# Gate and up of a feed-forward stage: one 512-column product for the high weights

## The chip, the core and the metric

The kernel runs on one core of a Trainium2 chip. The metric is the device time of one launch in microseconds, a median over runs. Lower is better.

## What is computed

A block with a state-space branch, attention and 32 experts (the first part), and then four layers, each with a mixer and a SwiGLU feed-forward stage. D is 1024, there are 256 tokens, and the hidden width is 2816. The change touches the four feed-forward stages alone:

```
def _swiglu(xn, w_gate, w_up, w_down):
    return (jax.nn.silu(xn @ w_gate) * (xn @ w_up)) @ w_down

for i in range(4):
    ...                                   # mixer: m
    x = x + _rms(m, g[1])
    f = _swiglu(_rms(x, g[2]), ffn_w_gate[i], ffn_w_up[i], ffn_w_down[i])
    x = x + _rms(f, g[3])
```

Everything is in 32 bits. The late products split each operand into a high part (rounded to the type fp32r) and a low part (the rest), and add three products: high weight with high input, high weight with low input, low weight with high input.

## The kernel before

**Layout.** Channels lie on the 128 partitions, tokens (256) along the free dimension. x is 8 chunks of 128 x 256. A piece of weights is 128 x 2048, 1 MB, and holds 16 blocks of 128 x 128. PSUM has 8 banks of 512 columns; `halves(b)` sees bank b as two outputs of 256 columns.

**A feed-forward stage** (`ffn`, L897) takes 33 pieces. For each index i of 11 (256 hidden channels) there is a gate piece, an up piece and a down piece; the order is gate 1, up 1, gate 2, up 2, down 1, and from then on gate i+1, up i+1, down i. The middle eight indices run in a hardware loop of two each (`FFN_TRIPS`), the last pieces are gate 11, up 11, down 10, down 11. `hidden_pair` (L901) makes gate and up: for each of the 8 input chunks k and both output halves m it calls `product` (L451), three products of 256 columns into one half of a bank:

```
mm(out, w[0], a[0], start=start, stop=False, **more)
mm(out, w[0], a[1], start=False, stop=False, **more)
return mm(out, w[1], a[0], start=False, stop=stop, **more)
```

Gate i goes to bank 4 or 5 in turn, up i to 6 or 7; the down pieces add into banks 0 to 3. Each product loads its weight block itself. After the first gate piece TensorE sums the squares of x (`x_sums`, L471), from which ACT makes `rstd_x`.

**Engines beside TensorE.** SP loads pieces into a ring of six slots, piece n when piece n-6 has been read (`late`). ACT makes the high part of a piece (`late_first`, L1152), DVE the low part from it (`low_part`, L361, called by `late_second`), four pieces ahead. Between these, in a fixed order, they treat the hidden values: DVE scales gate with `rstd_x` (`f_g`), ACT takes silu (`gate_silu`, L1287), DVE scales up (`f_u`) and multiplies (`f_a`), ACT makes the high part of that (`hidden_first`, L1291) and DVE the low part (`hidden_second`, semaphore `f_low`), on which the down piece waits. For each index ACT's order is: high part of a piece, silu, high part, hidden high, high part; DVE's: low part, f_g, low part, f_u and f_a, low part, hidden low. Ahead of the stage, `add_result` on DVE and `next_input` on ACT (L1173) make the input's parts `h2` chunk by chunk, and the first gate piece waits for each chunk.

**Memory.** `h2` has its high part in `h_parts` and its low part at 4096 of the arena; `squares` lies at 2048 of the arena.

Of the kernel before, what the change touches and what calls it, by code (L numbers as in the profile page):

```python
# [16 lines left out]
T = 256  # L17
# [179 lines left out]
def build(nc, io):  # L197
    with ExitStack() as ctx:
# [127 lines left out]
        h2 = (shaped(h_parts[:], (KC, T)), parts(4096, KC, T))  # L326
# [19 lines left out]
        f_a = view(7680, 2, T)  # L346
        f_parts = tuple(parts(8192 + 1024 * n, 2, 2, T) for n in range(2))
# [95 lines left out]
        def _(pe):  # L443
# [17 lines left out]
            def norm_sums(b):  # L461

                k = at["norm"]
                for c in range(KC):
                    if c % 2 == 0:
                        pe.wait_ge(sem("squares_ready"), 4 * k + c // 2 + 1)
                    last = mm(psum[:, b, 0:T], ones, squares[:, c, :], start=c == 0, stop=c == KC - 1)  # L467
                last.then_inc(sem("norm_sums"), 1)
                at["norm"] += 1
# [313 lines left out]
            norm_sums(4)  # L783
# [50 lines left out]
            def diff_attention(ready):  # L834
# [57 lines left out]
                for head in range(HEADS2):  # L892
                    pe.wait_ge(sem("o2_ready"), head + 1)
                    for c in range(2):
                        last = mm(halves(2, 2)[:, head, :], ones, squares[:, 2 * head + c, :], start=c == 0, stop=c == 1)
                last.then_inc(sem("o2_sums"), 1)
            def ffn(layer):  # L897
# [44 lines left out]
            for layer in range(LAYERS):  # L942
                ready = (sem("late_h_low"), MIXER_H[layer] * KC)
                if layer == 1:
                    norm_sums(5)
# [12 lines left out]
                norm_sums(2)  # L958
                ffn(layer)
                norm_sums(4)  # L960
# [5 lines left out]
        def _(act):  # L966
# [13 lines left out]
            def squares_of(src, waits=None):  # L980
                if at["norm"] >= 1:
                    act.wait_ge(sem("norm_sums"), at["norm"])
                for n in range(4):
# [3 lines left out]
                    go(squares[:, cols, :], src[:, cols, :], ACT.Square).then_inc(sem("squares_ready"), 1)  # L987

            def x_squares():

                at["x"] += 1
                squares_of(x, (sem("x_ready"), KC * (at["x"] - 1)))
# [176 lines left out]
            for j in range(4):  # L1169
                go(squares[:, 2 * j:2 * j + 2, :], halves(j), ACT.Square).then_inc(sem("squares_ready"), 1)  # L1170
            rstd_of(4)

            def next_input(scales):  # L1173
# [3 lines left out]
                for c in range(KC):  # L1177
                    act.wait_ge(sem("x_ready"), KC * (at["x"] - 1) + c + 1)
                    go(h2[0][:, c, :], x[:, c, :], ACT.Copy, scale=scales[:, c:c + 1]).then_inc(sem("late_h_high"), 1)
                    if c % 2:  # L1180
                        go(squares[:, c - 1:c + 1, :], x[:, c - 1:c + 1, :], ACT.Square).then_inc(sem("squares_ready"), 1)

            def result_out(i, done, scales=None):
# [3 lines left out]
                if scales is None:  # L1187
                    go(squares[:, 2 * i:2 * i + 2, :], halves(i % 2), ACT.Square).then_inc(sem("squares_ready"), 1)
                    go(mixed[:, 2 * i:2 * i + 2, :], halves(i % 2), ACT.Copy).then_inc(sem("pair_out"), 1)
                    return  # L1190
                for fn, dst, signal in ((ACT.Square, squares, "squares_ready"), (ACT.Copy, mixed, "pair_out")):
# [4 lines left out]
            for layer in range(LAYERS):  # L1196
# [13 lines left out]
                elif layer == 1:  # L1210
                    x_squares()
# [8 lines left out]
                else:  # L1220
# [23 lines left out]
                    for i in range(HEADS2 * TT):  # L1244
# [8 lines left out]
                        if i % TT == TT - 1:  # L1253
# [3 lines left out]
                            go(squares[:, 2 * head:2 * head + 2, :], o2[:, 2 * head:2 * head + 2, :], ACT.Square  # L1257
# [28 lines left out]

                def gate_silu(i):  # L1287
# [7 lines left out]
                for i in range(2):  # L1295
                    late_first(n + AHEAD + 2 * i)
                    gate_silu(it + 1 + i)
                    late_first(n + AHEAD + 2 * i + 1)
                    hidden_first(it + 1 + i, i)
                late_first(n + AHEAD + 4)  # L1300
                m = n + FFN_HEAD + AHEAD
                with act.Fori(0, FFN_TRIPS) as i:
                    for buf in range(2):
                        late_first(m + 3 * buf, i)
                        gate_silu(i * 2 + (it + 3 + buf))
                        late_first(m + 3 * buf + 1, i)
                        hidden_first(i * 2 + (it + 3 + buf), buf)
                        late_first(m + 3 * buf + 2, i)
                m = n + FFN_PIECES
                late_first(m)  # L1310
                gate_silu(it + FC2)
                late_first(m + 1)
                hidden_first(it + FC2, 0)
# [4 lines left out]
                for j in range(4):  # L1318
# [4 lines left out]
                    go(squares[:, 2 * j:2 * j + 2, :], halves(j), ACT.Square).then_inc(sem("squares_ready"), 1)  # L1323
# [761 lines left out]
```

## Time and profile before

| | us |
|---|---|
| median of 3 runs | 2685.67 |
| lowest, highest | 2682.75, 2690.65 |
| the profiled execution | 2689.83 |
| its span, first to last instruction | 2688.0 |
| mean granted TensorE clock | 0.957 |
| TensorE busy (share of the span) | 2476.4 (92%) |
| DVE busy, ACT busy | 1124.7, 691.9 |

The first product of the four layers starts at 1460.90 us of the span, and the four feed-forward stages fill most of what follows. A timeline row gives the start, the duration, the engine, the line, the operation, and output<-inputs with their shapes; in brackets stands how long the engine was idle before it, and what ended that. A product's duration overlaps the next one's: the pace is read from the distance of the starts. PE is TensorE's product, PEld its weight load.

### The profile page before, as it was taken

How to read it: one execution, taken by the hardware profiler on the slowest of the kernel's cores; microseconds unless marked ns; L12 is line 12 of the kernel's file. 1: busy time of each engine (PE TensorE's matmuls, PEld its weight loads, DVE VectorE, ACT ScalarE, POOL GpSimd, SP SyncE). 2: the span in 40 equal slices, each digit the busy share in tenths (PEclk: the TensorE clock that was granted, in tenths of full speed). 3: DMA queues.
4: the chain of work that ended last, by engine and by line, in shares of the span. 5: the costliest groups of instructions: out<-in, count | busy, mean ns of one | idle time of the engine just before them, and what ended most of it. 6: DMA issues, size and time to landing. Idle time of an engine off the chain costs nothing.

```text
span 2688.0 us, 37887 instructions
## 1 busy us (share of the span) xinstructions
PE 2476.4 (92%) x15414; PEld 1799.1 (67%) x15414; DVE 1124.7 (42%) x1599; ACT 691.9 (26%) x855; POOL 95.1 (4%) x52
## 2 busy tenths in 40 slices
PE   7866888999999999999997999969999899998998
PEld 4544764444444444444445989959999789988998
DVE  5876312111111111111114755565555455566553
ACT  1122120000000000000003344344343444344432
POOL 0123000000000000000000000000000000000000
PEclk9877987999999999999998999989999899999999
DMA  7333326999999999999995444524544145444552
GB/s 314 110 111 147 121 84 274 422 422 422 422 422 422 422 422 422 422 421 422 422 422 236 171 158 180 187 78 169 187 172 157 59 145 187 176 154 141 173 187 79
DMA packets 93764, 676.41 MB, mean 252 GB/s; under 512 B 10452, under 2 KB 11096, under 8 KB 11640
## 3 DMA queue, kind: packets, MB, share of 16 engines
q1 hardware_dynamic: 92592, 673.36, 63.4%
q10 hardware_dynamic: 1096, 1.97, 0.2%
q8 instruction: 55, 0.90, 0.1%
q14 instruction: 21, 0.17, 0.0%
HBM read 674.23 MB, written 1.06 MB: 251 GB/s over the span
## 4 chain that ended last, share of the span: by engine, by line
PE 74%; DMA 13%; DVE 9%; ACT 2%; issue 1%; POOL 0%; SPq 0%; DVEq 0%; ACTq 0%; POOLq 0%
PE psum L715 13%; PE psum L453 13%; PE psum L454 12%; PE psum L455 12%; DMA ring<-in_w_exp 12%; PE psum L740 5%; DVE arena L1373 3%; PE psum L699 3%; PE psum L513 3%; PE psum L467 2%; DVE arena L1379 2%; PE psum L750 2%; PE psum L633 1%; PE psum L494 1%; PE psum L603 1%; DVE arena_parts L1379 1%
## 5 line engine op out<-in xcount | busy, mean ns | idle before, releaser
L454 PE MATMUL psum<-arena_parts,ring_parts 128*128 128x256 f32 x2832 | 809.8, 286 | 0.0
L453 PE MATMUL psum<-h_parts,ring_parts 128*128 128x256 f32 x1920 | 555.7, 289 | 39.3 <-DVE arena_parts L1379 38.2
L454 PEld LDWEIGHTS psum<-arena_parts,ring_parts 128*128 128x128 f32 x2832 | 552.8, 195 | 0.2
L364 DVE TENSOR_TENSOR ring_parts<-ring,ring_parts 128x2048 fp32r<-128x2048 f32 x181 | 414.4, 2291 | 322.5 <-ACT ring_parts L1162 317.2
L455 PE MATMUL psum<-h_parts,ring_parts 128*128 128x256 f32 x1920 | 548.3, 286 | 0.0
L715 PE MATMUL psum<-ring,arena 128*64 128x512 f32 x2176 | 486.4, 597 | 5.4 <-DMA ring<-in_w_exp 5.3
L453 PEld LDWEIGHTS psum<-h_parts,ring_parts 128*128 128x128 f32 x1920 | 374.0, 195 | 49.3 <-issue 32.0
L455 PEld LDWEIGHTS psum<-h_parts,ring_parts 128*128 128x128 f32 x1920 | 374.1, 195 | 0.0
L1162 ACT ACTIVATE ring_parts<-ring 128x2048 fp32r<-128x2048 f32 x181 | 342.2, 1903 | 70.8 <-DMA ring<-in_w_mix 47.0
L715 PEld LDWEIGHTS psum<-ring,arena 128*64 128x64 f32 x2176 | 152.1, 137 | 296.6 <-issue 296.6
L1376 DVE TENSOR_SCALAR arena<-psum 128x512 f32<-128x512 f32 x68 | 47.0, 691 | 627.9 <-ACT arena L1141 469.8
L453 PE MATMUL psum<-arena_parts,ring_parts 128*128 128x256 f32 x912 | 261.9, 287 | 29.7 <-DVE arena_parts L1373 29.7
L455 PE MATMUL psum<-arena_parts,ring_parts 128*128 128x256 f32 x912 | 261.0, 286 | 0.0
L740 PE MATMUL psum<-ring,arena 128*64 128x512 f32 x1088 | 241.0, 595 | 0.0
L453 PEld LDWEIGHTS psum<-arena_parts,ring_parts 128*128 128x128 f32 x912 | 178.3, 196 | 31.3 <-issue 25.7
L740 PEld LDWEIGHTS psum<-ring,arena 128*64 128x64 f32 x1088 | 75.1, 137 | 161.7 <-issue 161.7
L455 PEld LDWEIGHTS psum<-arena_parts,ring_parts 128*128 128x128 f32 x912 | 178.2, 195 | 0.0
L699 PEld LDWEIGHTS psum<-arena 128*128 128x128 f32 x1120 | 130.9, 196 | 31.1 <-issue 31.1
L699 PE MATMUL psum<-arena 128*128 128x64 f32 x1120 | 135.8, 281 | 3.4 <-DVE arena L1376 3.4
L1135 ACT ACTIVATE arena<-psum 128x512 f32<-128x512 f32 x35 | 20.9, 597 | 374.4 <-PE psum L699 374.4
L1373 DVE TENSOR_TENSOR arena<-psum,rstd_x 128x512 f32<-128x512 f32 x112 | 77.0, 688 | 86.4 <-PE psum L455 86.4
L1373 DVE TENSOR_TENSOR arena<-arena 128x512 f32<-128x512 f32 (+6 forms) x160 | 103.5, 651 | 9.8 <-ACT arena L1006 4.7
(245 smaller groups left out, 1977.4 us busy)
## 6 DMA issues: line engine op xcount, KB each, us to landing
ring<-in_w_exp SPq DMA_DIRECT2D x408, 1024.0 KB, 19.0
ring<-in_w_ffn SPq DMA_DIRECT2D x132, 1024.0 KB, 4.8
ring<-in_w_mix SPq DMA_DIRECT2D x49, 1024.0 KB, 4.8
ring<-in_w_ada SPq DMA_DIRECT2D x24, 1024.0 KB, 5.1
ring<-in_w_in SPq DMA_DIRECT2D x16, 1024.0 KB, 6.2
ring<-in_w_out SPq DMA_DIRECT2D x4, 1024.0 KB, 4.8
ring<-in_w_attn SPq DMA_DIRECT2D x2, 1024.0 KB, 4.7
ring<-in_w_ssm SPq DMA_DIRECT2D x2, 1024.0 KB, 5.5
```

The lines of the kernel that those rows point to most:

```text
L364: return engine.tensor_tensor(ring_parts[:, s, :], ring[:, s, :], ring_parts[:, RAW + s, :], ALU.subtract)
L453: mm(out, w[0], a[0], start=start, stop=False, **more)
L454: mm(out, w[0], a[1], start=False, stop=False, **more)
L455: return mm(out, w[1], a[0], start=False, stop=stop, **more)
L467: last = mm(psum[:, b, 0:T], ones, squares[:, c, :], start=c == 0, stop=c == KC - 1)
L513: last = mm(halves(n % 2)[:, m, :], blocks_of(slot)[:, m * KC + k, :], src[:, k, :], start=k == 0, stop=k == KC - 1)
L699: last = mm(psum[:, 6, m * CAP:(m + 1) * CAP], h_tok[:, t, m * P:(m + 1) * P], sel[:, t, :], start=t == 0, stop=t == TT - 1)
L715: last = mm(psum[side(half), bank, :], hg[:, 4 * n + k, :], w[half][:, k * HALF:(k + 1) * HALF], start=False, stop=n == 1 and k == 3, skip ...
L740: last = mm(psum[side(half), 7, :], act_t[:, f % 4, f // 4, :], w[:, (2 * k + half) * HALF:(2 * k + half + 1) * HALF], start=f == 0, stop= ...
L1162: go(ring_parts[:, RAW + s, :], ring[:, s, :], ACT.Copy).then_inc(late_high, 1)
L1373: return v.tensor_tensor(out, a, b, op)
L1379: return v.scalar_tensor_tensor(out=out, in0=a, scalar=s, in1=b, op0=op0, op1=op1)
```

## The change

The two parts of the input now lie behind each other, `h2` high at 2048 and low at 4096, so that `h2_both` sees both. For each block of gate and up the high weight block is multiplied with both at once, one product of 512 columns (two runs of 256) into a whole bank, left half the high input's result, right half the low input's; the low weight block adds 256 columns into the left half. So a gate piece fills banks 4 and 5 (m is the bank), an up piece 6 and 7, and each of them waits for the reader of the piece before it. On the way out ACT copies the right halves of both banks to `f_low`, DVE adds the left halves to it, and then multiplies with `rstd_x` as before. The squares of the late norms go to the place where `h2`'s high part was (`squares2` is `h`). Products of the mixers and of the down pieces stay as they are.

```
-        h2 = (shaped(h_parts[:], (KC, T)), parts(4096, KC, T))
+        h2 = (parts(2048, KC, T), parts(4096, KC, T))
+        h2_both = parts(2048, 2, KC, T)
+        squares2 = h
...
+        f_low = view(10240, 2, T), view(10752, 2, T)
...
                     for half in range(2):
                         w = late_weights(n + half, more)
+                        if not first or layer > 0:
+                            pe.wait_ge(sem(("f_g_ready", "f_u_ready")[half]), i - 1)
                         for k in range(KC):
...
                             for m in range(2):
-                                last = product(halves(4 + 2 * half + buf)[:, m, :], two(w, m * KC + k), two(h2, k),
-                                               start=k == 0 and m == 0, stop=k == KC - 1, skip_group_check=True)
+                                out = psum[:, 4 + 2 * half + m, :]
+                                mm(out, w[0][:, m * KC + k, :], h2_both[:, :, k, :], start=k == 0, stop=False,
+                                   skip_group_check=True)
+                                last = mm(out[:, 0:T], w[1][:, m * KC + k, :], h2[0][:, k, :], start=False,
+                                          stop=k == KC - 1, skip_group_check=True)
...
+                def low_halves(which, count):
+                    act.wait_ge(late, count)
+                    go(f_low[which], psum[:, 4 + 2 * which:6 + 2 * which, T:2 * T], ACT.Copy
+                       ).then_inc(sem(("f_g_low", "f_u_low")[which]), 1)
...
                 for i in range(2):
                     late_first(n + AHEAD + 2 * i)
+                    low_halves(0, n + 2 * i + 1)
                     gate_silu(it + 1 + i)
                     late_first(n + AHEAD + 2 * i + 1)
+                    low_halves(1, n + 2 * i + 2)
                     hidden_first(it + 1 + i, i)
...
-                def gate_pair(count, i, buf):
-                    dve.wait_ge(late, count)
-                    tt(f_g, halves(4 + buf), along(rstd_x[:], 2), ALU.mult).then_inc(sem("f_g_ready"), 1)
...
+                def gate_pair(i):
+                    dve.wait_ge(sem("f_g_low"), i)
+                    tt(f_g, psum[:, 4:6, 0:T], f_low[0], ALU.add).then_inc(sem("f_g_sum"), 1)
+                    dve.wait_ge(sem("f_g_sum"), i)
+                    tt(f_g, f_g, along(rstd_x[:], 2), ALU.mult).then_inc(sem("f_g_ready"), 1)
+
+                def up_pair(i):
+                    dve.wait_ge(sem("f_u_low"), i)
+                    tt(f_u, psum[:, 6:8, 0:T], f_low[1], ALU.add).then_inc(sem("f_u_sum"), 1)
+                    dve.wait_ge(sem("f_u_sum"), i)
+                    tt(f_u, f_u, along(rstd_x[:], 2), ALU.mult).then_inc(sem("f_u_ready"), 1)
                     dve.wait_ge(sem("f_u_ready"), i)
                     dve.wait_ge(sem("f_s_ready"), i)
                     tt(f_a, f_s, f_u, ALU.mult).then_inc(sem("f_ready"), 1)
```

The loop body and the tail of ACT and DVE get the same two calls in the same places.

DVE at the start of layer 0's feed-forward stage, before (L364 is the low part of a piece, L1373 the helper of its two-tensor operations):

```order
L364 TENSOR_TENSOR ring_parts<-ring,ring_parts 128x2048 [waits late_weights_high,rstd_ready,x_ready]
L1373 TENSOR_TENSOR arena<-psum,rstd_x 128x512 [waits late_pieces_read]
L364 TENSOR_TENSOR ring_parts<-ring,ring_parts 128x2048 [waits late_weights_high]
L1373 TENSOR_TENSOR arena<-psum,rstd_x 128x512 [waits late_pieces_read]
L1373 TENSOR_TENSOR arena<-arena 128x512 [waits f_s_ready,f_u_ready]
L1373 TENSOR_TENSOR arena_parts<-arena,arena_parts 128x512 [waits f_high]
```

DVE at the same place of the changed kernel, where the helpers are L367 and L1392:

```order
L367 TENSOR_TENSOR ring_parts<-ring,ring_parts 128x2048 [waits late_weights_high,rstd_ready,x_ready]
L1392 TENSOR_TENSOR arena<-psum,arena 128x512 [waits f_g_low]
L1392 TENSOR_TENSOR arena<-arena,rstd_x 128x512 [waits f_g_sum]
L367 TENSOR_TENSOR ring_parts<-ring,ring_parts 128x2048 [waits late_weights_high]
L1392 TENSOR_TENSOR arena<-psum,arena 128x512 [waits f_u_low]
L1392 TENSOR_TENSOR arena<-arena,rstd_x 128x512 [waits f_u_sum]
L1392 TENSOR_TENSOR arena<-arena 128x512 [waits f_s_ready,f_u_ready]
L1392 TENSOR_TENSOR arena_parts<-arena,arena_parts 128x512 [waits f_high]
```

Each operation that read PSUM and scaled has become an add from PSUM and a scaling behind it; the rest of the order stays.

TensorE in layer 0 from the last product of gate 1 over the x sums (L476) into up 1, before:

```order
L455 MATMUL psum<-h_parts,ring_parts 128x256
L476 MATMUL psum<-diagonal,con 128x256 [waits squares_added]
L453 MATMUL psum<-h_parts,ring_parts 128x256 [waits late_weights_low]
L454 MATMUL psum<-arena_parts,ring_parts 128x256
L455 MATMUL psum<-h_parts,ring_parts 128x256
```

TensorE in the changed kernel, from the last two products of up 1 into gate 2 (L915 is the 512-column product, L917 the 256-column one):

```order
L915 MATMUL psum<-arena_parts,ring_parts 128x512
L917 MATMUL psum<-arena_parts,ring_parts 128x256
L915 MATMUL psum<-arena_parts,ring_parts 128x512 [waits f_g_ready,late_weights_low]
L917 MATMUL psum<-arena_parts,ring_parts 128x256
L915 MATMUL psum<-arena_parts,ring_parts 128x512
```

A block has gone from three rows to two, and gate 2 begins with a wait for `f_g_ready` that its first product did not have.

## Rows read from the trace of the kernel before

**Rows 1.** The page, part 1: busy time, share of the span, instructions by engine
```profile
PE 2476.4 (92%) x15414; PEld 1799.1 (67%) x15414; DVE 1124.7 (42%) x1599; ACT 691.9 (26%) x855; POOL 95.1 (4%) x52
```

**Rows 2.** Windows of layer 1's feed-forward: length, busy us (instructions) by engine, clock, DMA
```profile
core 0: us, PE busy (x) PEld busy (x) DVE busy (x) ACT busy (x) POOL busy (x), PEclk, DMA share, GB/s
1850.00:1900.00 50.00, 50.00 (x419) 50.00 (x418) 31.82 (x24) 23.91 (x18) 0.00 (x0) 1.00 0.50 174
```

**Rows 3.** Timeline, PE, 256-column products of layer 1's gate: start us, duration us
```profile
1991.74 0.28 PE L455 MATMUL psum<-h_parts,ring_parts 128*128 128x256 f32 x1
...
1993.66 0.28 PE L453 MATMUL psum<-h_parts,ring_parts 128*128 128x256 f32 x1
```

**Rows 4.** Timeline, PE, 512-column products of layer 2's value projection
```profile
2067.50 0.39 PE L454 MATMUL psum<-ring_parts,h_parts 128*128 128x512 f32 x1
...
2088.83 0.39 PE L455 MATMUL psum<-ring_parts,arena_parts 128*128 128x512 f32 x1
```

**Rows 5.** Timeline, PE, end of layer 0's first gate piece and start of up
```profile
1580.30 0.59 PE L476 MATMUL psum<-diagonal,con 128*128 128x256 f32 x2
...
1580.84 0.28 PE L454 MATMUL psum<-arena_parts,ring_parts 128*128 128x256 f32 x1
```

**Rows 6.** Timeline, ACT, the first passes of layer 0's feed-forward
```profile
1583.16 1.91 ACT L1162 ACTIVATE ring_parts<-ring 128x2048 fp32r<-128x2048 f32 x1
1588.14 0.63 ACT L1289 ACTIVATE arena<-arena 128x512 f32<-128x512 f32 x1 [3.06 <-DVE arena L1373]
1588.67 1.90 ACT L1162 ACTIVATE ring_parts<-ring 128x2048 fp32r<-128x2048 f32 x1
1594.25 0.63 ACT L1293 ACTIVATE arena_parts<-arena 128x512 fp32r<-128x512 f32 x1 [3.68 <-DVE arena L1373]
1594.79 1.90 ACT L1162 ACTIVATE ring_parts<-ring 128x2048 fp32r<-128x2048 f32 x1
```

**Rows 7.** Timeline, DVE, the same stretch
```profile
1585.21 2.29 DVE L364 TENSOR_TENSOR ring_parts<-ring,ring_parts 128x2048 fp32r<-128x2048 f32 x1 [5.79 <-ACT ring_parts L1162]
1587.42 0.68 DVE L1373 TENSOR_TENSOR arena<-psum,rstd_x 128x512 f32<-128x512 f32 x1
1590.60 2.29 DVE L364 TENSOR_TENSOR ring_parts<-ring,ring_parts 128x2048 fp32r<-128x2048 f32 x1 [2.50 <-ACT ring_parts L1162]
1592.81 0.68 DVE L1373 TENSOR_TENSOR arena<-psum,rstd_x 128x512 f32<-128x512 f32 x1
1593.53 0.69 DVE L1373 TENSOR_TENSOR arena<-arena 128x512 f32<-128x512 f32 x1
1594.92 0.69 DVE L1373 TENSOR_TENSOR arena_parts<-arena,arena_parts 128x512 fp32r<-128x512 f32 x1 [0.70 <-ACT arena_parts L1293]
1596.79 2.29 DVE L364 TENSOR_TENSOR ring_parts<-ring,ring_parts 128x2048 fp32r<-128x2048 f32 x1 [1.18 <-ACT ring_parts L1162]
```

**Rows 8.** Groups by line, layers 1 to 3: busy us, mean ns, idle before
```profile
L1188 ACT ACTIVATE arena<-psum 128x512 f32<-128x512 f32 x8 | 4.8, 597 | 26.6 <-PE psum L455 26.6
```

**Rows 9.** Timeline, ACT and DVE, the same place in layer 1
```profile
1825.57 1.28 ACT L1283 ACT_TABLE_LOAD   x1 [1.41 <-issue]
1828.91 2.29 DVE L364 TENSOR_TENSOR ring_parts<-ring,ring_parts 128x2048 fp32r<-128x2048 f32 x1 [7.17 <-ACT ring_parts L1162]
```

**Rows 10.** Timeline, PE, a wait inside a conv mixer and the products behind it
```profile
1537.75 0.28 PE L455 MATMUL psum<-arena_parts,ring_parts 128*128 128x256 f32 x1
1540.41 0.40 PE L453 MATMUL psum<-arena_parts,ring_parts 128*128 128x256 f32 x1 [2.38 <-DVE arena_parts L1373]
...
1540.82 0.42 PE L455 MATMUL psum<-arena_parts,ring_parts 128*128 128x256 f32 x1
...
1543.80 0.41 PE L454 MATMUL psum<-arena_parts,ring_parts 128*128 128x256 f32 x1
```

**Rows 11.** Windows around that wait, columns as in rows 2
```profile
1541.00:1542.00 1.00, 1.00 (x7) 1.00 (x6) 0.36 (x2) 1.00 (x1) 0.00 (x0) 0.50 0.08 16
...
1544.00:1545.00 1.00, 1.00 (x11) 1.00 (x10) 0.47 (x1) 0.00 (x0) 0.00 (x0) 0.97 0.00 0
```

**Rows 12.** Timeline, PE, the same wait in layer 3; a window behind it
```profile
2448.54 0.56 PE L453 MATMUL psum<-arena_parts,ring_parts 128*128 128x256 f32 x1 [2.37 <-DVE arena_parts L1373]
...
2449.00:2450.00 1.00, 1.00 (x7) 1.00 (x7) 0.49 (x2) 1.00 (x1) 0.00 (x0) 0.50 0.06 16
```

More of the change, by code:

```diff
@@ L466, in norm_sums @@
                         pe.wait_ge(sem("squares_ready"), 4 * k + c // 2 + 1)
-                    last = mm(psum[:, b, 0:T], ones, squares[:, c, :], start=c == 0, stop=c == KC - 1)
+                    last = mm(psum[:, b, 0:T], ones, src[:, c, :], start=c == 0, stop=c == KC - 1)
                 last.then_inc(sem("norm_sums"), 1)
@@ L782, in _ @@
             scatter(blocks)
-            norm_sums(4)
+            norm_sums(4, squares2)
             def late_weights(n, more=0):
@@ L894, in diff_attention @@
                     for c in range(2):
-                        last = mm(halves(2, 2)[:, head, :], ones, squares[:, 2 * head + c, :], start=c == 0, stop=c == 1)
+                        last = mm(halves(2, 2)[:, head, :], ones, squares2[:, 2 * head + c, :], start=c == 0, stop=c == 1)
                 last.then_inc(sem("o2_sums"), 1)
@@ L978, in rstd_of, with squares_of @@
                 go(dst[:], lnv[:], ACT.Exp, scale=-0.5).then_inc(sem("rstd_ready"), 1)
-            def squares_of(src, waits=None):
+            def squares_of(src, waits=None, dst=squares):
                 if at["norm"] >= 1:
@@ L1169, in _ @@
             for j in range(4):
-                go(squares[:, 2 * j:2 * j + 2, :], halves(j), ACT.Square).then_inc(sem("squares_ready"), 1)
+                go(squares2[:, 2 * j:2 * j + 2, :], halves(j), ACT.Square).then_inc(sem("squares_ready"), 1)
             rstd_of(4)
@@ L1180, in next_input @@
                     if c % 2:
-                        go(squares[:, c - 1:c + 1, :], x[:, c - 1:c + 1, :], ACT.Square).then_inc(sem("squares_ready"), 1)
+                        go(squares2[:, c - 1:c + 1, :], x[:, c - 1:c + 1, :], ACT.Square).then_inc(sem("squares_ready"), 1)
             def result_out(i, done, scales=None):
@@ L1187, in result_out @@
                 if scales is None:
-                    go(squares[:, 2 * i:2 * i + 2, :], halves(i % 2), ACT.Square).then_inc(sem("squares_ready"), 1)
+                    go(squares2[:, 2 * i:2 * i + 2, :], halves(i % 2), ACT.Square).then_inc(sem("squares_ready"), 1)
                     go(mixed[:, 2 * i:2 * i + 2, :], halves(i % 2), ACT.Copy).then_inc(sem("pair_out"), 1)
                     return
-                for fn, dst, signal in ((ACT.Square, squares, "squares_ready"), (ACT.Copy, mixed, "pair_out")):
+                for fn, dst, signal in ((ACT.Square, squares2, "squares_ready"), (ACT.Copy, mixed, "pair_out")):
                     for c in (2 * i, 2 * i + 1):
@@ L1256, in _ @@
                             step(go(o2[:, 2 * head:2 * head + 2, :], halves(head % 2), ACT.Copy))
-                            go(squares[:, 2 * head:2 * head + 2, :], o2[:, 2 * head:2 * head + 2, :], ACT.Square
+                            go(squares2[:, 2 * head:2 * head + 2, :], o2[:, 2 * head:2 * head + 2, :], ACT.Square
                                ).then_inc(sem("o2_ready"), 1)
@@ L1322, in _ @@
                         act.wait_ge(late, n + FFN_PIECES)
-                    go(squares[:, 2 * j:2 * j + 2, :], halves(j), ACT.Square).then_inc(sem("squares_ready"), 1)
+                    go(squares2[:, 2 * j:2 * j + 2, :], halves(j), ACT.Square).then_inc(sem("squares_ready"), 1)
                 rstd_of(4)
@@ L1353, in _ @@
                 pool.wait_ge(sem("squares_ready"), 4 * k + 2)
[L1354 removed]
+                adds(nc.gpsimd.tensor_tensor(square_sum, squares2[:, 0:2, :], squares2[:, 2:4, :], ALU.add))
                 for n in (2, 3):
                     pool.wait_ge(sem("squares_ready"), 4 * k + n + 1)
[L1357 removed]
+                    adds(nc.gpsimd.tensor_tensor(square_sum, square_sum, squares2[:, 2 * n:2 * n + 2, :], ALU.add))
                 nc.gpsimd.tensor_tensor(square_sum[:, 0, :], square_sum[:, 0, :], square_sum[:, 1, :], ALU.add
@@ L1910, in _ @@
                 it = layer * FC2
-                def gate_pair(count, i, buf):
-                    dve.wait_ge(late, count)
-                    tt(f_g, halves(4 + buf), along(rstd_x[:], 2), ALU.mult).then_inc(sem("f_g_ready"), 1)
-                def up_pair(count, i, buf):
-                    dve.wait_ge(late, count)
-                    tt(f_u, halves(6 + buf), along(rstd_x[:], 2), ALU.mult).then_inc(sem("f_u_ready"), 1)
+                def gate_pair(i):
[8 more added lines that the diff above has]
+                    tt(f_u, f_u, along(rstd_x[:], 2), ALU.mult).then_inc(sem("f_u_ready"), 1)
                     dve.wait_ge(sem("f_u_ready"), i)
```

34 lines of the change are left out of this document (18 added, 16 removed).

## Prediction

> **What bounds the kernel now.** I read the page first, then the dense part of a feed-forward stage, then its two ends. TensorE is busy for 92% of the span [rows 1]. In the middle of a feed-forward stage it is busy 50.00 of 50 us at full clock, while DVE works 32 us and ACT 24 us of the same 50 [rows 2]: nobody keeps TensorE waiting there, and the time of the stage is the sum of its products. A 256-column product starts every 0.120 us: 16 steps lie between the two starts shown, 1.92 us [rows 3]. A piece of 16 weight blocks has 48 such products, 5.76 us, and one index i (gate, up and the down piece of the index before) takes 17.28 us. So only a shorter product stream shortens the middle, and only a late operand lengthens it.
>
> **What one block of gate or up costs.** The same product with 512 columns stands in the trace too, with parts of the same type: 94 steps in 21.33 us, 0.2269 us each [rows 4]. Two of 256 columns cost 0.2400. A straight line through both sizes gives 0.0131 to 0.0133 us for each product whatever its width, and the rest by columns. Now a block costs 3 x 0.120 = 0.360 us, afterwards 0.2269 + 0.120 = 0.347, a saving of 0.0131 us. The columns are the same 768; what goes is one product's fixed part and one weight load out of three. The load was never what paced: one is fitted under every 0.120 us now. A piece falls from 5.76 to 5.55 us and one index from 17.28 to 16.86. The trace has no product whose moving operand is two runs of 256 columns from two places, nor one of 512 followed by one of 256. Its price lies between the straight line (0.347) and no gain at all (0.360); I take the line, to which the row of 512 is nearest. At half clock nothing is saved: there 256 columns take 0.213 us, which is their columns alone (14 steps from 1540.82 to 1543.80) [rows 10].
>
> The Trainium skill (TensorE: Matmul & The Clock Gate, section "Wait — 56ns, not 53.3ns?") gives a fixed part of about 2.5 ns for each product at full clock and none at half clock. The trace agrees at half clock and differs at full clock, where the two widths leave 13 ns. By the page the saving for each block would be a fifth of mine.
>
> **Where the saving counts.** There are 4 layers x 22 pieces of gate and up x 16 blocks = 1408 blocks, 18.4 us if all counted. The first gate piece of a layer is fed chunk by chunk by DVE and saves nothing. Up 1, gate 2 and up 2 lie ahead of the new waits, and their ends are set by DVE, see below. The 18 pieces from gate 3 to up 11 count in full: 18 x 16 x 0.0131 = 3.8 us a layer, 15.1 us in four.
>
> **The new waits.** Gate used banks 4 and 5 in turn, up 6 and 7. Now one gate piece fills 4 and 5 and one up piece 6 and 7, so gate i waits for f_g_ready of i-1, and up i for f_u_ready of i-1. Behind the waiting product everything of TensorE is queued, the down pieces too. From the third gate on, up and down lie between (11.3 us), and I find slack. Between gate 1 and gate 2 there is only up 1. Counted from the start of the x sums (1580.30 in layer 0) [rows 5]:
> - Up 1: its second product starts at 0.54, so gate 2 now starts at 0.54 - 0.12 + 5.76 = 6.18, and with shorter blocks would start at 0.42 + 5.55 = 5.97.
> - DVE's first low part of weights starts at 4.91 and the operation behind it at 7.12 [rows 7]. It waits for rstd_x and for ACT's high part, which starts at 2.86 [rows 6]; neither moves. The new ACT copy of the low half takes about 0.60 us, as an ACT copy of 512 columns from PSUM does [rows 8], starts behind that high part (some 4.8) and is done by 5.5, under DVE's 2.2 us. It costs nothing here.
> - At 7.12 the add stands where the multiply was. A dependent DVE operation of this size follows 0.72 later and lasts 0.69 [rows 7], so f_g_ready comes at 7.12 + 0.72 + 0.69 = 8.53, and TensorE starts about 0.14 later: gate 2 at 8.67, after a wait of 2.70 us.
> - Up 2: silu starts 0.04 after f_g, the next high part 0.53 behind it, DVE's low part 1.93 after that, the operation behind it 2.21 later [rows 6, 7]: the add at 8.57 + 0.53 + 1.93 + 2.21 = 13.24, f_u_ready at 14.65, up 2 at 14.79. Gate 2 ends at 8.67 + 0.11 for the first step after a wait + 5.55 = 14.33, so another 0.46 us.
> - Up 2 ends at 14.79 + 0.11 + 5.55 = 20.45 against 6.18 + 11.52 = 17.70: 2.75 us late.
>
> In layer 1 four DMA issues hold the table load back by 1.41 us; DVE's low part starts 6.31 after the x sums (1822.60) instead of 4.91 [rows 9]. There f_g_ready is later by 1.40 and up 2 ends 4.15 late; the wait is 4.1 us.
>
> **The clock.** Such a wait has a second price. A conv mixer has one of almost this length, between full streams of products: last start 1537.75, next 1540.41 [rows 10]. The granted clock stands at 0.50 behind it, that is the level of 1.2 GHz, and is back at 1544 [rows 11]: some 3.4 us in which 0.213 is paid for 0.120, about 1.5 us lost. The same wait in layer 3, 2.37 us idle, is followed by 0.50 too [rows 12]. In gate 2 that moves its end from 14.33 to 15.9, past f_u_ready, so the 0.46 is absorbed and about 1.0 us comes on top. Each of the four waits costs between 0 and 1.0 us more. The clock fell behind both waits shown, so I take 1.0 for all four.
>
> **The rest of the stage.** The round that ACT and DVE share for one index, from low part to low part, is now 2.21 + 0.72 + 0.72 + 0.53 + 1.93 + 2.21 + 0.72 + 0.72 + 0.72 + 0.54 + 2.00 + 2.21 + 0.69 = 15.9 us [rows 6, 7], of which the two added adds are 1.44. It stays under TensorE's 16.86, by 0.9 instead of 2.8 us. The copies of the low halves lie under DVE's 2.21. With it f_g of 2 is ready at 21.6 (gate 3 wants it at 26.2) and f_u of 2 at 27.7 (up 3 at 31.8), and from there the slack grows. At the end f_low of 11 must be there when down 10 is over, 5.55 + 5.76 = 11.3 us after gate 11's end. Copy 0.67, add and multiply 1.44, silu, high part and low part 0.53 + 1.93 + 2.21, then add, multiply, product, high and low of the hidden values come to 10.4. Cover is left, 0.9 us; were it gone, each us costs one in each of three layers. The moves of squares and of the high input part between buffers change no size, engine or wait: nothing.
>
> **Sum.** Layers 0, 2, 3: 2.75 + 1.0 - 3.8 = -0.05 each. Layer 1: 4.15 + 1.0 - 3.8 = +1.35. Together +1.2 us; with the clock never falling -2.8. The profiled execution took 2689.83 us (span 2688.0 and 1.8 around it), 4.2 above the median of 2685.67; the same change on the median gives 2686.9.
>
> **The rivals.**
> - The forecast: the first waits of each layer eat what the products save, 2683 to 2687. Chance 0.72.
> - Merging saves nothing, because the fixed part goes with each run of 256 columns that the product reads, and only the waits stay. It decides from the block: at 0.360 us the 15.1 us are missing and the time is 2702; at 0.355, 2696. For it: no row shows two runs in one product. Against it: the fixed part of the 512-column row is the same as that of 256 [rows 3, 4]. Slower; chance 0.08. By the 2.5 ns of the Trainium skill (same page and section) the saving would be 3 us in place of 15.1 and the time, as an estimate, 2699; the trace speaks against it.
> - The shared round becomes the bound. It decides from 16.86 us, 0.94 above my sum, and each 0.1 above costs 0.1 x 9 indices x 4 layers = 3.6 us. For it: it is a long chain, and PSUM reads of two banks in one add are not in the trace. Against it: a DVE operation from PSUM lasts 0.68, as from SBUF 0.69 [rows 7]. At 17.2 it would give 2699. Chance 0.08.
> - The waits are smaller, because DVE's order leaves more room than I read: gate 2 not waiting at all would leave the whole saving of some 17.5 us, 2668; half of the wait gone gives 2678. Against it: DVE waits 5.79 us for ACT ahead of that low part [rows 7], a chain from the x sums without a gap. Chance 0.07.
> - Other shifts of the clock at stage borders, a few us either way: 0.05.
>
> **How the numbers follow.** About 0.3% of this kernel, 8 us, is what a measurement can tell from no change, so the forecast counts as same. Same 0.78, slower 0.15 (both costly rivals, nearly whole), faster 0.07. The range runs from 2680, a few us below the case without clock falls, to 2697, into the cheaper half of the costly rivals; about 0.2 stay outside.
>
> **What would show it.** In the profile after: PE products of gate and up at 0.227 and 0.120 in turn; a PE wait of about 2.7 us (4.1 in layer 1) for DVE at the second gate piece of each layer, once for each layer; half clock behind it; no PE wait from gate 3 to down 11; each feed-forward from x sums to the last down product within 1.5 us of before. I am wrong if waits recur in every index, if a block takes 0.36, or if gate 2 starts less than 7 us after the x sums.

## The result and the profile after

The changed kernel takes 2696.43 us (7 runs, 2695.52 to 2701.16), against 2685.67 before: 10.8 us more. The ratio is 1.0038 with a 95% interval of 1.0027 to 1.0050, so it is slower by 0.3 to 0.5%. The prediction was 2686.9 with a range of 2680 to 2697. It took 8 us as the least that can be told from no change, so 10.8 us is the case that it called slower and gave a chance of 0.15.

From the page of the changed kernel, its span, part 1 and the clock of part 2:

```profile
span 2694.6 us, 35314 instructions
## 1 busy us (share of the span) xinstructions
PE 2475.4 (92%) x14006; PEld 1729.7 (64%) x14006; DVE 1183.1 (44%) x1687; ACT 738.5 (27%) x943; POOL 95.2 (4%) x52
...
PEclk9877887999999999999998999979999899999999
```

1408 products and weight loads fewer than in [rows 1], but TensorE is busy for almost the same time (2475.4 against 2476.4 us). The span grew by 6.6 us only, because the two profiled executions differ ahead of the changed stages: the first product of the four layers starts at 1456.29 instead of 1460.90 us, 4.6 us earlier, in code that the change leaves alone. From there on the stages can be compared one by one. A stage is counted from the start of its x sums to the start of the norm's first product behind down 11:

| us | layer 0 | layer 1 | layer 2 | layer 3 | sum |
|---|---|---|---|---|---|
| before | 184.74 | 184.74 | 184.74 | 184.75 | 738.97 |
| after | 186.62 | 189.08 | 186.49 | 186.52 | 748.71 |
| difference | +1.88 | +4.34 | +1.75 | +1.77 | +9.74 |

The three stretches between the stages (norms and mixers) took 353.92 before and 355.34 after, 1.4 more. Together 11.2 us; the medians differ by 10.8. That they agree so well is in part chance: 26 later runs of the kernel before had a median of 2687.44 us, from which the loss is 9.0. Nearly all of the 1.4 us lies in the first of the three stretches, which grew by 1.45 us, and there the granted clock (third from the end) is lower. First before, then after:

```profile
1765.04:1822.60 57.56, 29.38 (x147) 25.09 (x145) 39.86 (x73) 22.42 (x44) 5.38 (x4) 0.76 0.10 37
```

```profile
1762.32:1821.33 59.01, 30.58 (x130) 25.08 (x129) 39.87 (x73) 22.31 (x44) 5.39 (x4) 0.71 0.10 36
```

The waits of TensorE that the change added, over the whole span (line, releaser: us in total, times, longest; L915's other waits, 12 for L1398, are for the input chunks):

```profile
PE psum L915 <- DVE arena L1392: 11.8, 4, 4.4
```

L915 is the 512-column product. There are four such waits, one a layer, 11.8 us in all; L1392 is the helper that makes f_g and f_u. There is no fifth: none at up 2, none from gate 3 on. In layer 0 TensorE's x sums and the first product of gate 2 stand so:

```profile
1575.70 0.59 PE L479 MATMUL psum<-diagonal,con 128*128 128x256 f32 x2
...
1584.38 0.76 PE L915 MATMUL psum<-arena_parts,ring_parts 128*128 128x512 f32 x1 [2.44 <-DVE arena L1392]
```

Gate 2 starts 8.68 us behind the x sums. DVE in the same stretch, to be laid beside [rows 7]:

```profile
1580.62 2.29 DVE L367 TENSOR_TENSOR ring_parts<-ring,ring_parts 128x2048 fp32r<-128x2048 f32 x1 [5.78 <-ACT ring_parts L1170]
1582.83 0.68 DVE L1392 TENSOR_TENSOR arena<-psum,arena 128x512 f32<-128x512 f32 x1
1583.55 0.69 DVE L1392 TENSOR_TENSOR arena<-arena,rstd_x 128x512 f32<-128x512 f32 x1
1586.73 2.29 DVE L367 TENSOR_TENSOR ring_parts<-ring,ring_parts 128x2048 fp32r<-128x2048 f32 x1 [2.49 <-ACT ring_parts L1170]
1588.94 0.68 DVE L1392 TENSOR_TENSOR arena<-psum,arena 128x512 f32<-128x512 f32 x1
1589.66 0.69 DVE L1392 TENSOR_TENSOR arena<-arena,rstd_x 128x512 f32<-128x512 f32 x1
1590.38 0.69 DVE L1392 TENSOR_TENSOR arena<-arena 128x512 f32<-128x512 f32 x1
```

The low part of weights starts 4.92 behind the x sums as before. At 1582.83 the add from PSUM stands where the multiply was, the multiply follows 0.72 later, and TensorE starts 0.14 after its end. ACT's copy of the low half (L1297) begins just ahead of DVE's low part and ends under it:

```profile
1578.57 1.92 ACT L1170 ACTIVATE ring_parts<-ring 128x2048 fp32r<-128x2048 f32 x1
1580.39 0.58 ACT L1297 ACTIVATE arena<-psum 128x512 f32<-128x512 f32 x1
```

Behind the wait the clock is at half (windows: us, busy by engine, granted clock third from the end), as in [rows 11]:

```profile
1585.00:1586.00 1.00, 1.00 (x5) 0.90 (x4) 0.00 (x0) 1.00 (x1) 0.00 (x0) 0.50 0.95 401
1588.00:1589.00 1.00, 1.00 (x8) 0.86 (x7) 1.00 (x2) 0.00 (x0) 0.00 (x0) 1.00 0.00 0
```

And in the middle of the stage TensorE is busy without a gap, as in [rows 2], DVE for 1.5 us more:

```profile
1850.00:1900.00 50.00, 50.00 (x329) 45.51 (x328) 33.31 (x30) 23.51 (x21) 0.00 (x0) 1.00 0.53 183
```

What is not as forecast is the pace of the products. Two steps of a block and then, 32 blocks later, the first product of the down piece:

```profile
1671.22 0.40 PE L915 MATMUL psum<-arena_parts,ring_parts 128*128 128x512 f32 x1
1671.46 0.28 PE L917 MATMUL psum<-arena_parts,ring_parts 128*128 128x256 f32 x1
1671.58 0.40 PE L915 MATMUL psum<-arena_parts,ring_parts 128*128 128x512 f32 x1
...
1682.54 0.28 PE L456 MATMUL psum<-arena_parts,ring_parts 128*128 128x256 f32 x1
```

Gate and up of one index take 11.32 us, 0.3535 us a block. The 512-column product is followed after 0.24 (0.237 on average over this index), not after 0.227 [rows 4], the 256-column one after 0.12 (0.117 on average).

### The profile page after: what moved, and what is told of

It is laid out like the page before. It is cut to its first block, busy times and chain, and to the rows that moved or that the text cites. A ratio compares the mean times of both kernels' runs of the same rounds, so it can differ in the third digit from the quotient of the medians.

```text
span 2694.6 us, 35314 instructions
## 1 busy us (share of the span) xinstructions
PE 2475.4 (92%) x14006; PEld 1729.7 (64%) x14006; DVE 1183.1 (44%) x1687; ACT 738.5 (27%) x943; POOL 95.2 (4%) x52
## 4 chain that ended last, share of the span: by engine, by line
PE 74%; DMA 12%; DVE 10%; ACT 3%; issue 1%; POOL 0%; SPq 0%; ACTq 0%; DVEq 0%; POOLq 0%
PE psum L718 13%; PE psum L915 12%; DMA ring<-in_w_exp 11%; PE psum L456 6%; PE psum L458 6%; PE psum L457 6%; PE psum L917 6%; PE psum L743 6%; DVE arena L1392 4%; PE psum L702 3%; PE psum L516 3%; PE psum L470 2%; DVE arena L1398 2%; PE psum L753 2%; PE psum L636 1%; PE psum L606 1%
## 5 line engine op out<-in xcount | busy, mean ns | idle before, releaser
L367 DVE TENSOR_TENSOR ring_parts<-ring,ring_parts 128x2048 fp32r<-128x2048 f32 x181 | 414.2, 2291 | 321.5 <-ACT ring_parts L1170 311.6
L915 PE MATMUL psum<-arena_parts,ring_parts 128*128 128x512 f32 x1408 | 517.8, 409 | 33.8 <-DVE arena_parts L1398 21.4
L456 PE MATMUL psum<-arena_parts,ring_parts 128*128 128x256 f32 x1424 | 412.2, 289 | 46.8 <-DVE arena_parts L1392 29.7
L457 PE MATMUL psum<-arena_parts,ring_parts 128*128 128x256 f32 x1424 | 408.7, 287 | 0.0
L458 PE MATMUL psum<-arena_parts,ring_parts 128*128 128x256 f32 x1424 | 408.4, 287 | 0.0
L917 PE MATMUL psum<-arena_parts,ring_parts 128*128 128x256 f32 x1408 | 402.2, 286 | 0.0
L915 PEld LDWEIGHTS psum<-arena_parts,ring_parts 128*128 128x128 f32 x1408 | 272.2, 193 | 106.7 <-issue 31.3
L456 PEld LDWEIGHTS psum<-arena_parts,ring_parts 128*128 128x128 f32 x1424 | 279.1, 196 | 54.1 <-issue 39.4
L457 PEld LDWEIGHTS psum<-arena_parts,ring_parts 128*128 128x128 f32 x1424 | 279.4, 196 | 0.1
L458 PEld LDWEIGHTS psum<-arena_parts,ring_parts 128*128 128x128 f32 x1424 | 279.1, 196 | 0.0
L917 PEld LDWEIGHTS psum<-arena_parts,ring_parts 128*128 128x128 f32 x1408 | 273.9, 195 | 0.1
L1392 DVE TENSOR_TENSOR arena<-arena 128x512 f32<-128x512 f32 (+6 forms) x160 | 103.5, 651 | 9.4 <-ACT arena L1014 4.2
L1395 DVE TENSOR_SCALAR arena<-psum,arena 128x256 f32<-128x256 f32 x34 | 16.4, 484 | 201.6 <-PE psum L733 201.6
```

The costliest lines, as they stand in the source:

```text
L367: return engine.tensor_tensor(ring_parts[:, s, :], ring[:, s, :], ring_parts[:, RAW + s, :], ALU.subtract)
L915: mm(out, w[0][:, m * KC + k, :], h2_both[:, :, k, :], start=k == 0, stop=False, skip_group_check=True)
L917: last = mm(out[:, 0:T], w[1][:, m * KC + k, :], h2[0][:, k, :], start=False, stop=k == KC - 1, skip_group_check=True)
L1392: return v.tensor_tensor(out, a, b, op)
```

## Experiments

All start from the changed kernel. "Stages" is the sum of the four stages as above (before 738.97, after 748.71), "between" the three stretches between them. The kernel before, measured beside them, had medians of 2687.44 and 2687.8 us, and 2687.28 in the one run beside the last two.

**Without the waits.** Indices 1 and 2 in the old form, with the old banks:

```
-                        if not first or layer > 0:
+                        if (first and layer > 0) or not old:
                             pe.wait_ge(sem(("f_g_ready", "f_u_ready")[half]), i - 1)
...
+                                if old:
+                                    last = product(halves(4 + 2 * half + buf)[:, m, :], two(w, m * KC + k), two(h2, k),
+                                                   start=k == 0 and m == 0, stop=k == KC - 1, skip_group_check=True)
+                                    continue
...
-                hidden_pair(n0, it + 1, 0, first=True)
-                hidden_pair(n0 + 2, it + 2, 1)
+                hidden_pair(n0, it + 1, 0, first=True, old=True)
+                hidden_pair(n0 + 2, it + 2, 1, old=True)
```

with the reads of these two indices on DVE as before the change and no copies on ACT for them.

> Indices 1 and 2 of each layer are multiplied and read as in the kernel before (three products of 256, banks 4/5 and 6/7 in turn), indices 3 to 11 as in the changed kernel, so gate 2 and up 2 have no new wait. Theory 1 (the waits ahead of gate 2 and up 2 and the half clock behind them are what costs; a block of the changed form takes 0.3533 us instead of 0.360): no PE wait at gate 2, each feed-forward stage from x sums to the last down product 184.7 - 18 x 16 x 0.0067 = 182.8 us, total 2685.7 - 7.7 = 2678 us, ratio 0.997. Rival (the added reads and copies slow the whole stage, or the mixers got longer by the moved buffers): stages stay above 184.7 and the total at 2690 or more.

Measured: 2676.3 us (2674.4 to 2677.15), ratio 0.9956 [0.9942, 0.9970]. No wait of TensorE stands between x sums and down 11 in any layer. The stages take 182.82, 182.83, 182.82 and 182.82 us, the expected figure to 0.02; between them 352.9. So against the changed kernel the start of a stage had cost 3.80, 6.25, 3.67 and 3.70 us, 17.4 in all, and what is left of the change (narrow blocks, adds, copies, waits that never wait) is a gain of 1.92 us a layer. The rival, that the added reads and copies slow the stage, is refuted: they stand in nine of eleven indices here.

**The clock alone.** Products that nobody reads, in the place of the wait:

```
+                for _ in range(34 if layer == 1 else 20):
+                    mm(psum[:, 0, 0:T], h2[0][:, 0, 0:P], h2[0][:, 1, :], start=True, stop=True)
                 hidden_pair(n0 + 2, it + 2, 1)
```

> The changed kernel, with products that nobody reads between up 1 and gate 2 (20 of 256 columns, 34 in layer 1), so that TensorE is busy where it waited; the waits themselves stay. Theory 1 says: gate 2 starts where it started (8.7 us behind the x sums, 10.5 in layer 1), the clock stays at 1.00, a wait of about 0.5 us appears ahead of up 2, and each stage is shorter by 1.0 us (2 in layer 1): total 2696.4 - 5 = 2691 us. Rival (the half clock is hidden by the wait ahead of up 2 and costs nothing): total unchanged, 2696.

Measured: 2690.5 us (2687.7 to 2694.1), ratio 1.0012 [1.0003, 1.0022]. In layer 0 the added products and gate 2:

```profile
1586.11 2.54 PE L937 MATMUL psum<-arena_parts 128*128 128x256 f32 x20
1588.82 0.47 PE L915 MATMUL psum<-arena_parts,ring_parts 128*128 128x512 f32 x1 [0.16 <-DVE arena L1394]
```

A window behind it, columns as above, clock at 1.00:

```profile
1589.00:1590.00 1.00, 1.00 (x7) 0.87 (x7) 0.00 (x0) 1.00 (x2) 0.00 (x0) 1.00 1.00 426
```

Gate 2 starts at 8.69 behind the x sums, where it started without them, with an idle time of 0.16 us. The wait that was expected ahead of up 2 came too, 0.24 to 0.33 us. The stages take 185.65, 188.30, 185.65 and 185.55, shorter by 0.97, 0.78, 0.84 and 0.97. So the half clock costs 0.8 to 1.0 us in layers 0, 2 and 3. In layer 1 another thing hides a part of it; ACT's table load and gate 2 there, the x sums at 1822.89:

```profile
1827.12 1.28 ACT L1293 ACT_TABLE_LOAD   x1 [2.68 <-issue]
...
1834.23 0.47 PE L915 MATMUL psum<-arena_parts,ring_parts 128*128 128x512 f32 x1 [1.14 <-DVE arena L1394]
```

The table load came after 2.68 us of issuing DMAs, where the changed kernel has 1.89 for the same four. Gate 2 started at 11.34 behind the x sums instead of 10.55, at full clock. 0.78 saved in spite of 0.79 lost makes 1.6 for the half clock, an estimate that takes the later table load as unrelated; 2 was expected. The stretches between the stages took 351.9 us, 3.4 less than after. The median fell by 5.9 us, but the stages by 3.6 only: that it came so near the expected 2691 is partly luck.

The runs below hold a second test of this, which nobody planned. In four stages (layer 0 of e_grouped, e_banks and e_samebank, layer 3 of e_samebank) the clock stayed at full behind the same wait. Layer 0 of e_banks, the first product of gate 2 and a window behind it:

```profile
1584.60 0.47 PE L922 MATMUL psum<-arena_parts,ring_parts 128*128 128x512 f32 x1 [2.54 <-DVE arena L1400]
```

```profile
1585.00:1586.00 1.00, 1.00 (x8) 0.86 (x7) 0.00 (x0) 1.00 (x2) 0.00 (x0) 1.00 1.01 426
```

Up 2 then waits 0.24 us, as with the added products, and the stage takes 185.65 us, against 186.53 and 186.52 in layers 2 and 3 of the same run, where the clock fell: 0.9 us again. In e_samebank it is 184.14 twice against 185.15.

**One run of 512 columns instead of two of 256.** High and low part of a chunk side by side:

```
-        h2 = (parts(2048, KC, T), parts(4096, KC, T))
-        h2_both = parts(2048, 2, KC, T)
+        h2_both = parts(2048, KC, 2 * T)
+        h2 = (h2_both[:, :, 0:T], h2_both[:, :, T:2 * T])
...
-                                mm(out, w[0][:, m * KC + k, :], h2_both[:, :, k, :], start=k == 0, stop=False,
+                                mm(out, w[0][:, m * KC + k, :], h2_both[:, k, :], start=k == 0, stop=False,
```

> The changed kernel with the high and low part of each input chunk side by side, so that the 512-column product reads one run of 512 columns instead of two of 256. Theory 2a (the second run costs the missing 6.6 ns of a block): a block takes 0.3467 us everywhere, total 2696.4 - 4 x 18 x 16 x 0.0066 = 2689 us. Theory 2b (something else, such as products of two widths in turn): a block stays at 0.3533, total 2696.

Measured: 2695.95 us (2693.6 to 2701.7), ratio 1.0033 [1.0024, 1.0043]. Gate and up of one index, from the first product to that of the down piece:

```profile
1671.16 0.40 PE L915 MATMUL psum<-arena_parts,ring_parts 128*128 128x512 f32 x1
...
1682.47 0.28 PE L456 MATMUL psum<-arena_parts,ring_parts 128*128 128x256 f32 x1
```

11.31 us, nothing changed. Reading two runs costs nothing, and theory 2a is refuted.

**The 16 wide products first, then the 16 narrow ones.**

```
-                        for k in range(KC):
-                            if first and half == 0:
+                        if first and half == 0:
+                            order = [(k, m, p) for k in range(KC) for m in range(2) for p in range(2)]
+                        else:
+                            order = [(k, m, p) for p in range(2) for k in range(KC) for m in range(2)]
+                        for k, m, p in order:
...
-                            for m in range(2):
...
+                            if p == 0:
                                 mm(out, w[0][:, m * KC + k, :], h2_both[:, :, k, :], start=k == 0, stop=False,
                                    skip_group_check=True)
+                            else:
```

where p says which of the two products is made: 0 the wide one (512 columns), 1 the narrow one (256). The first gate piece keeps its order.

> The changed kernel with the products of a piece in another order: first the 16 of 512 columns, then the 16 of 256 (the first gate piece of a layer excepted). Theory 2b (widths in turn cost 6.6 ns a block): 512-column steps 0.2267, 256-column steps 0.120, a piece 5.55 us, total 2689 us. Theory 2a (two runs cost it): 512-column steps 0.2333, a piece 5.65 us, total 2696.

Measured: 2685.4 us (2682.4 to 2692.8), ratio 0.9997 [0.9987, 1.0008]. One piece, the wide ones, the narrow ones, and the down piece behind them:

```profile
1692.22 3.82 PE L919 MATMUL psum<-arena_parts,ring_parts 128*128 128x512 f32 x16
1695.87 2.08 PE L922 MATMUL psum<-arena_parts,ring_parts 128*128 128x256 f32 x16
1697.78 0.28 PE L456 MATMUL psum<-arena_parts,ring_parts 128*128 128x256 f32 x1
```

16 wide products in 3.65 us (0.228), 16 narrow ones in 1.91 (0.119), 5.56 together against 5.66. An index takes 11.13. That is the line through the two widths, which the prediction drew, all but 1 ns. The stages fell by 7.0 to 741.68 us, where 4 x 18 x 0.095 = 6.8 was due. That agreement is partly chance, for by layers it is 2.59, 1.18, 1.52 and 1.74: in layer 0 the clock did not fall, and in layer 1 gate 2 waited 5.19 us instead of 4.40. The stretches between took 350.9, 4.4 less, and the total is 4 us under the expected 2689. A comparison without such waits stands at the end of this section.

**What in the order costs.** Three further orders of the same products. Pairs: 512, 512, 256, 256, banks in turn.

```
                             for m in range(2):
...
+                                mm(psum[:, 4 + 2 * half + m, :], w[0][:, m * KC + k, :], h2_both[:, :, k, :],
+                                   start=k == 0, stop=False, skip_group_check=True)
+                            for m in range(2):
+                                last = mm(psum[:, 4 + 2 * half + m, 0:T], w[1][:, m * KC + k, :], h2[0][:, k, :],
+                                          start=False, stop=k == KC - 1, skip_group_check=True)
```

> The changed kernel with the products of each chunk as 512, 512, 256, 256 (banks in turn) instead of 512, 256, 512, 256 (each pair into one bank). Theory 2b (each change of width costs): half the changes, a block at about 0.350 us. Theory 2c (a 256-column product right behind the 512-column one into the same bank costs): none of these are left, 0.3467 us. If neither, 0.3533.

Swapped: in each block the narrow product first.

```
+                                mm(out[:, 0:T], w[1][:, m * KC + k, :], h2[0][:, k, :], start=k == 0, stop=False,
+                                   skip_group_check=True)
+                                last = mm(out, w[0][:, m * KC + k, :], h2_both[:, :, k, :], start=False,
+                                          stop=k == KC - 1, skip_group_check=True)
```

> The changed kernel with the low weight's 256 columns ahead of the high weight's 512 in each block. Theory 2b (widths in turn): as many changes as in the changed kernel, 0.3533 us a block. Theory 2c' (only a 256-column product behind a 512-column one in the same columns costs; here it is behind one in the other bank): 0.3467 us.

Pairs took 11.15 us, less than a price on each change of width would give, and swapped 11.32. The next two let the widths and the banks vary apart. Widths one by one, neighbours in different banks:

```
+                            order = [(k, (j + p) % 2, p) for j in range(2) for k in range(KC) for p in range(2)]
```

> The changed kernel with the products of a piece in this order: for each chunk the 512 columns of half 0 and the 256 of half 1, then for each chunk the 512 of half 1 and the 256 of half 0. Widths alternate at every step as in the changed kernel, but (but for one step of 32) neighbours never go to the same bank. Theory 2b (one width behind the other, singly, costs): gate and up of an index 11.31 us, a block 0.3533. Theory 2c (neighbours of unlike width in one bank cost): 11.13 us, 0.348.

Pairs of one width, neighbours in the same bank:

```
+                            order = [(2 * q + r, m, p) for m in range(2) for q in range(KC // 2) for p in range(2) for r in range(2)]
```

> The changed kernel with 512, 512, 256, 256 columns as in e_pairs, but all four in the same bank (two chunks of one half). Theory 2b: as in e_pairs, gate and up of an index 11.15 us. Theory 2c (neighbours in one bank cost): 11.3 us or more.

The first product of an index and that of the down piece behind its up piece, in the order pairs, swapped, banks apart, pairs in one bank:

```profile
1672.19 0.63 PE L914 MATMUL psum<-arena_parts,ring_parts 128*128 128x512 f32 x2
...
1683.34 0.28 PE L456 MATMUL psum<-arena_parts,ring_parts 128*128 128x256 f32 x1
```

```profile
1670.92 0.28 PE L915 MATMUL psum<-arena_parts,ring_parts 128*128 128x256 f32 x1
...
1682.24 0.28 PE L456 MATMUL psum<-arena_parts,ring_parts 128*128 128x256 f32 x1
```

```profile
1670.46 0.40 PE L922 MATMUL psum<-arena_parts,ring_parts 128*128 128x512 f32 x1
...
1681.78 0.28 PE L456 MATMUL psum<-arena_parts,ring_parts 128*128 128x256 f32 x1
```

```profile
1668.96 0.63 PE L922 MATMUL psum<-arena_parts,ring_parts 128*128 128x512 f32 x2
...
1680.11 0.28 PE L456 MATMUL psum<-arena_parts,ring_parts 128*128 128x256 f32 x1
```

W is a wide product, N a narrow one. The last column is a single execution but for the last row, and bears little.

| order of widths | banks of neighbours | gate and up, us | block, us | one run, us |
|---|---|---|---|---|
| W N W N (after) | same, then other | 11.32 | 0.3535 | 2696.4 |
| N W N W (swapped) | same, then other | 11.32 | 0.3535 | 2696.4 |
| W N W N | always other | 11.32 | 0.3535 | 2696.2 |
| W W N N | always other | 11.15 | 0.3484 | 2687.3 |
| W W N N | always same | 11.15 | 0.3484 | 2687.5 |
| 16 W, 16 N | other | 11.13 | 0.3478 | 2685.4 (median) |

The bank makes no difference in either order (theory 2c is refuted), nor does it matter which width comes first in a block. What costs 5 to 6 ns a block is a strict alternation of one wide and one narrow product; in pairs it is almost gone. It isn't the change between high and low weights either: the kernel before makes it in two of three steps, at 0.120 us each [rows 3]. A cost for each change of width, as 2b had it, would have left half of it in pairs. It left a tenth. Why single alternation is slower, the runs don't say. Nor is it a fixed property of the order: four of the pieces of the changed kernel (up 2 of layers 1 and 3, gate 3 and up 3 of layer 2) run at 0.347 in the same order, and the next ones at 0.3535 again. e_contig, e_swap and e_banks have a few such pieces too, partly in other layers; none comes later than up 3. So alternation can run at the line's pace, and what tips it stays open.

**Both repairs.** Indices 1 and 2 in the old form, the others with the wide products first.

> Both repairs together: indices 1 and 2 in the old form (no wait at gate 2), indices 3 to 11 in the new form with the 16 products of 512 columns ahead of the 16 of 256. Theory 1 and 2b together: each stage 184.7 - 18 x (5.76 - 5.56) = 181.1 us, total 2676.3 - 4 x 1.7 = 2669 us, ratio 0.993 to the kernel before. Rival (the gain of the grouped order came from other places, such as the phase of the clock at stage borders): stages stay at 182.8 and the total at 2676.

Measured: 2673.4 us (2667.1 to 2676.7), ratio 0.9939 [0.9927, 0.9952]. Each stage takes 181.26 us where 181.1 was expected, and 1.56 less than with the old order (e_old12): this is what the order is worth where no wait and no half clock enter, 6.2 us in all. The total is 4 above the expected 2669. In its profiled execution (2676.6) the first x sums of the feed-forward come at 1580.77 instead of 1575.28, and the stretches between the stages take 354.1 instead of 352.9; neither is in changed code. This kernel is 0.6% faster than the one before, and the fastest measured here.

## Why the prediction was right and wrong

The total: 2696.4 lies in the range, but the likeliest case, no change, is not what came, and that it lies inside at all is partly luck. The upper end, 2697, was set for the two costly rivals, and neither mechanism came; what moved the time there is a mis-sized saving and two smaller terms. By steps:

- **Bound and middle of the stage**: right. No wait stands from gate 3 to down 11, DVE and ACT keep up, and the copies are hidden. e_old12 shows that the adds, copies and waits of nine indices cost nothing.
- **The saving of a block**: the step that failed. The prediction's sum took 0.347 us, from a line through rows of products that all had the same width as their neighbours [rows 3, 4], and kept 0.360 as the other end. It came to 0.3535, the middle: 0.0067 saved, not 0.0131, 1.92 us a layer instead of 3.8. That is 7.4 (four times 3.77 - 1.92) of the 8.5 us by which the stages missed (9.7 instead of 1.2). The line itself held for products in groups: e_grouped 0.3478.
- **Merging saves nothing**, the rival: its mechanism is refuted by e_contig. At 0.355 us a block it said 2696, close to what came, but partly by chance: by its own sum the measured 0.3535 gives 2694.4, and the rest are layer 1 and the stretches between the stages.
- **The wait at gate 2**: right. Forecast 8.67 us behind the x sums, measured 8.68; f_u_ready forecast at 14.65, measured 1589.66 + 0.69 - 1575.70 = 14.65.
- **The clock**: right in the main. It fell behind all four waits; 1.0 us was forecast for each, and e_fill shows 0.8 to 1.0, in layer 1 an estimated 1.6. That it fell in all of them was not certain: over all runs that keep the waits it fell behind 17 of 21 waits of 2.44 to 2.54 us. The text's bounds, 0 to 1.0 us a wait, cover both outcomes but for layer 1. The wait ahead of up 2 was absorbed, as the text said. The end of up 2 was forecast 3.75 us late; layer 0 shows 3.80.
- **Layer 1**: too small by 1.1 us. Up 2 ended 6.25 late, not 5.15. The table load of ACT came after 1.89 us of issuing, not 1.41 [rows 9], so gate 2 started at 10.55 instead of 10.1, and the half clock cost 1.6 instead of 1.0: behind the longer wait the products stayed at the slow pace from 1831.88 to 1836.9, 5.0 us, where [rows 10, 11] had 3.4. ACT's table load and the first product of gate 2 in layer 1 (timeline, x sums at 1821.33):

```profile
1824.78 1.28 ACT L1291 ACT_TABLE_LOAD   x1 [1.89 <-issue]
...
1831.88 0.76 PE L915 MATMUL psum<-arena_parts,ring_parts 128*128 128x512 f32 x1 [4.40 <-DVE arena L1392]
```

- **The shared round as a bound**: did not come, as forecast. Its sum was 15.9 us; from low part to low part DVE takes 15.99 in layer 0 (1609.74 to 1625.73), under the index of 17.07.
- **Other shifts**: 1.4 us more between the stages here. The runs that start from the changed kernel show how large this term is, with the same code there: from 350.8 to 355.5 us, on both sides of the 353.92 before, so the moved buffers need not be its cause. The text gave it a chance of 0.05 and "a few us", without a place in the sum; with the first part, which differs by some 5 us between executions, it is as large as the effect that was to be found.

The fixed part of 13 ns that the trace showed stood up against the 2.5 ns of the Trainium skill (TensorE: Matmul & The Clock Gate, section "Wait — 56ns, not 53.3ns?"): by the page's figure the merging would, as an estimate, save 2.5 ns a block, and e_grouped saves 12 (0.360 - 0.3478).

## What to carry to other kernels

Where two products are merged into a wide one, the price of the new stream need not be the sum of the prices of its products in streams of one width: put equal widths next to each other, at least in pairs. A buffer that is given up (here two banks in turn) is paid where nothing lies between two uses, at the start of a stage, and there a wait of about 2.5 us mostly cost a further us by the clock; leave the first iterations in the form that needs no wait. And what happens at the borders of stages shifts a kernel of this kind by several us either way, so compare stages, from event to event, before totals.

## What the runs showed of the hardware

- 512- and 256-column products of type fp32r in strict turn take 0.3535 us a pair, in pairs of one width 0.3484, in groups of 16 0.3478. The PSUM bank of the neighbours and the number of runs in the moving operand make no difference. A few pieces in strict turn, all near the start of a stage, ran at 0.347.
- Of 21 idle times of 2.44 to 2.54 us in a full stream 17 were met by the half clock, 1.2 GHz, for 3.4 us, and four were not, in the same place of the stage; all seven of 4.00 to 5.19 us were met by it. With products in the gap the clock stayed at 2.4 GHz. The half clock of a stage start costs 0.8 to 1.0 us where a wait behind it absorbs a part.
